# Eight expert blocks move from the one-hot steps to the routing, and VectorE makes the low parts of 39 blocks

## The reference, cut to what matters

```python
def peer_block(xb, w_q, sub_keys, expert_u, expert_v):     # xb: normed tokens x 1024
    q = (xb @ w_q).reshape(T, 8, 2, 128)
    s = jnp.einsum('thpd,hpkd->thpk', q, sub_keys)          # two lists of 128 keys for each head
    sv, si = lax.top_k(s, 16)
    cand = (sv[:, :, 0, :, None] + sv[:, :, 1, None, :]).reshape(T, 8, 256)
    cidx = (si[:, :, 0, :, None] * 128 + si[:, :, 1, None, :]).reshape(T, 8, 256)
    top_s, pos = lax.top_k(cand, 16)                        # the routing: 16 experts a head
    eidx = jnp.take_along_axis(cidx, pos, axis=-1)
    gate = jax.nn.softmax(top_s, axis=-1)
    u = jnp.take(expert_u, eidx, axis=0)
    act = jax.nn.gelu(jnp.einsum('thkd,td->thk', u, xb))
    v = jnp.take(expert_v, eidx, axis=0)
    return jnp.einsum('thk,thkd->td', gate * act, v)
```

## Time and profile before

| | us |
|---|---|
| median of 3 runs | 2854.35 (2854.25 to 2856.07) |
| the profiled execution, its own time | 2859.36 |
| its span, from the first to the last instruction | 2857.5 |
| TensorE busy | 2697.9 |
| VectorE busy | 2213.6 |
| GpSimd busy | 1298.4 |
| mean granted TensorE clock, share of full speed | 0.981 |

### The profile page before, as it was taken

One profiled execution on the slowest core, in us unless ns is written; L12 is line 12 of the kernel. 1 busy time (PEld: TensorE's weight loads), 2 busy tenths in 40 slices (PEclk: granted clock), 3 DMA queues, 4 the chain that ended last, 5 costly groups with the idle time before them and its releaser, 6 DMA issues.

```text
span 2857.5 us, 36824 instructions
## 1 busy us (share of the span) xinstructions
PE 2697.9 (94%) x14355; PEld 2240.7 (78%) x14355; DVE 2213.6 (77%) x3528; ACT 1212.2 (42%) x1802; POOL 1298.4 (45%) x827
## 2 busy tenths in 40 slices
PE   8889999999999999999999799999999999998987
PEld 4567777767767788787788799999888898777765
DVE  3688888876878977657569998883777788888975
ACT  4234444443533466733334446564333333233333
POOL 2233333332224544204444455555676766667730
PEclk9999999999999999999999899999999999999998
DMA  7321111134422221023233346677999999899961
GB/s 280 103 70 53 52 52 52 52 125 151 144 67 74 82 67 45 30 83 117 82 103 103 119 133 225 209 249 278 360 377 361 376 341 340 321 337 322 325 246 37
DMA packets 163165, 496.12 MB, mean 174 GB/s; under 512 B 15152, under 2 KB 50992, under 8 KB 162864
## 3 DMA queue, kind: packets, MB, share of 16 engines
q1 hardware_dynamic: 126128, 359.53, 37.2%
q0 software_dynamic: 36864, 134.23, 12.7%
HBM read 443.90 MB, written 49.81 MB: 173 GB/s over the span
## 4 chain that ended last, share of the span: by engine, by line
PE 50%; DVE 24%; DMA 12%; ACT 7%; issue 4%; POOL 3%; SPq 1%; DVEq 0%; ACTq 0%; POOLq 0%
PE ps L804 12%; PE ps L806 12%; PE ps L805 12%; DMA ex<-in_ev,small 4%; DMA ex<-in_urow,small 4%; DVE ex L1806 3%; PE ps L1212 2%; DVE ex L2589 2%; DVE ex L2603 2%; DVE ex L2610 2%; DVE wsp L1806 2%; PE ps L977 2%; POOL ex L2843 1%; PE ps L997 1%; DMA ring<-in_ev 1%
## 5 line engine op out<-in xcount | busy, mean ns | idle before, releaser
L2697 POOL TENSOR_TENSOR wsp<-ring,wsp 128x1024 fp32r<-128x1024 f32 x219 | 568.2, 2600 | 867.5 <-ACT wsp L1306 839.7
L804 PE MATMUL ps<-hT,wsp 128*128 128x512 f32 (+1 forms) x2040 | 780.7, 383 | 38.0 <-POOL wsp L2697 20.0
L806 PE MATMUL ps<-hT,wsp 128*128 128x512 f32 (+1 forms) x2040 | 752.4, 369 | 0.0
L805 PE MATMUL ps<-hT,wsp 128*128 128x512 f32 (+1 forms) x2040 | 752.0, 369 | 0.0
L804 PEld LDWEIGHTS ps<-hT,wsp 128*128 128x128 f32 x2040 | 388.4, 190 | 109.1 <-issue 32.1
L806 PEld LDWEIGHTS ps<-hT,wsp 128*128 128x128 f32 x2040 | 387.8, 190 | 46.7
L805 PEld LDWEIGHTS ps<-hT,wsp 128*128 128x128 f32 x2040 | 388.9, 191 | 44.0 <-issue 5.0
L1306 ACT ACTIVATE wsp<-ring 128x1024 fp32r<-128x1024 f32 x317 | 331.9, 1055 | 158.0 <-PE ps L806 80.0
L804 PE MATMUL ps<-ex 128*128 128x512 f32 x588 | 233.7, 397 | 30.4 <-DVE ex L1806 26.9
L2855 POOL DMA_INDIRECT ex<-in_ev,small x128 | 190.5, 1488 | 110.1 <-DVE ex L2610 93.1
L2855 POOL DMA_INDIRECT ex<-in_urow,small x128 | 197.1, 1540 | 88.6 <-DVE small L2603 77.3
(11 more groups left out here) (431 smaller groups left out, 4909.3 us busy)
## 6 DMA issues: line engine op xcount, KB each, us to landing
ring<-in_eu SPq DMA_DIRECT2D x128, 512.0 KB
ring<-in_ev SPq DMA_DIRECT2D x128, 512.0 KB
ring<-in_ein SPq DMA_DIRECT2D x57, 512.0 KB
gd<-oh SPq DMA_DIRECT2D x6, 4096.0 KB, 14.0
ex<-gd SPq DMA_DIRECT2D x32, 768.0 KB
ring<-in_oin SPq DMA_DIRECT2D x39, 512.0 KB
ring<-in_ada SPq DMA_DIRECT2D x30, 512.0 KB
ex<-zd SPq DMA_DIRECT2D x20, 768.0 KB, 9.9
```

The lines of the kernel that those rows point to most:

```text
L804: pe.matmul(out, W[0], R[0], start=first, stop=False)
L805: pe.matmul(out, W[0], R[1], start=False, stop=False)
L806: return pe.matmul(out, W[1], R[0], start=False, stop=last)
L2697: pool.tensor_tensor(s[:, 1, :], raw_of(i), s[:, 0, :].bitcast(F32), ALU.subtract).then_inc(pool_done, G.step("lo", i))
```

## The change

1. Eight blocks move from the one-hot steps to the routing. Before, 4 stand ahead of the first `cand` and 4 in each token block; then 4 ahead of the first step and 2 in each of the 24 steps. Now 6 stand ahead of `cand`, then 5, 5, 6 and 6 in the token blocks (28 in all instead of 20); then 5 ahead of the first step, 1 in every step, and a second in 15 of the 24.
2. The low parts of units 33 to 71 of `expert_u` (39 units, those of the blocks among the steps) go from POOL to DVE.
3. The entry for `pre` in DVE's table calls `lo_to(n)` instead of `lo_to(n + 1)` for these blocks. The call of `split_to` in `walk` is as it was.

```diff
-SOFT = 4 + 4 * 4
-HOT = 4 + 48
+SOFT = 6 + 5 + 5 + 6 + 6
+HOT = 5 + 24 + 15
...
-    for _ in range(4):
+    for _ in range(6):
         pre()
     for blk in range(4):
         order.append(("cand", blk))
         pre()
         for part in range(4):
             order.append(("best", blk, part))
-            if part in (1, 3):
+            if part:
                 pre()
         order.append(("gates", blk))
         order.append(("decode", blk))
         order.append(("look", blk))
         pre()
+        if blk > 1:
+            pre()
         order.append(("sums", blk))
         order.append(("soft", blk))
     assert z[0] == SOFT
     order.append(("oh_begin",))
-    for _ in range(4):
+    for _ in range(5):
         pre()
     for tb in range(SD // TB):
         pre()
-        pre()
+        if tb % 8 in (1, 3, 5, 6, 7):
+            pre()
         order.append(("hot", tb))
...
-                    or name == "eu" and u < NPRE * JC)
+                    or name == "eu" and u < NPRE * JC and not SOFT + 5 <= u < SOFT + HOT)
...
-"pre": lambda j, n: lo_to(n + 1)
+"pre": lambda j, n: lo_to(n if SOFT + 5 <= j < SOFT + HOT else n + 1)
```

More of the change, by code:

```diff
@@ L2678, in vector_program @@
                   "pool_in": ahead_of, "mx_begin": mx_begin, "pool_ev": pool_ev, "bc": bc, "res": res, "vc": vc,
-                  "yms": yms, "wo": wo, "wq": ahead_of, "keys": keys, "pre": lambda j, n: lo_to(n + 1), "cand": cand_,
+                  "yms": yms, "wo": wo, "wq": ahead_of, "keys": keys, "pre": lambda j, n: lo_to(n if SOFT + 5 <= j < SOFT + HOT else n + 1), "cand": cand_,
                   "best": best, "gates": gates, "decode": decode, "look": look, "soft": soft, "hot": hot, "z": z, "v": v, "gd": gd, "gact": gact, "vl": vl, "vtr": vtr,
```

## The result

The changed kernel takes 2988.68 us (median of 4 runs, 2983.84 to 2999.28); the kernel before, run with it, 2855.21 (4 runs). The ratio is 1.047, with a 95% interval of 1.044 to 1.049: slower by some 133 us. Forecast were 3006 us and a range of 2950 to 3050.

What follows compares the result with a forecast made beforehand. TensorE was taken to bound the one-hot steps, with DVE just behind, and DVE parts of the routing. The terms -13.8 + 120 + 46 gave +152 us, so 3006 us, with a range of 2950 to 3050.

Steps and rivals of the forecast that it cites:

- term 1: In the routing: the eight moved blocks fill part of TensorE's lost time there, 13.8 us gained.
- term 2: One-hot steps: rows stand behind low parts on DVE, so PE waits 4.8 or 6.0 us, 23 times; 120 us lost.
- term 3: One-hot steps: PE resumes at a slow clock after each of 23 waits, 2.0 us each; 46 us lost.
- The rival on the other side: One-hot steps: rows come early enough, PE stays full and only the routing's gain is left; 2840 us, chance 4%.
- The one where the clock stays full: One-hot steps: the waits come but the clock is not slowed; +106 us, 2960 us, chance 16%, a mixture included.
- The one where it stays at half throughout: One-hot steps: the clock stays at half, work taken as 1.85 times as long; 3070 us, chance 8%.

Runs made afterwards that it cites:

- look0: Changed kernel with VectorE's lookahead behind a block taken off for units 33 to 71: ratio 0.9955 to the kernel before, median 2848.76 us.
- pool_lo: Changed kernel with all low parts of the early blocks back on GpSimd: ratio 0.9948 to the kernel before, median 2844.89 us.
- fill2: Changed kernel with 24 idle TensorE matmuls in each of the 24 steps, before the wait for the rows: ratio 1.0368 to the kernel before, median 2964.25 us.
- dve_only: Kernel before with the low parts of its blocks 24 to 71 on VectorE, no block moved: ratio 1.0474 to the kernel before, median 2996.34 us.
- look1: Changed kernel with VectorE's lookahead of one unit instead of two, table entry lo_to(n + 1) again: ratio 1.0036 to the kernel before, median 2868.84 us.

## Why the prediction was right, point by point

| | forecast | measured |
|---|---|---|
| routing (term 1) | -13.8 | -12.3 (`look0`), -12.8 (`pool_lo`) |
| waits at the steps (term 2) | 120 | 107.6 |
| slow clock behind them (term 3) | 46 | 35 |
| sum | 152 | 130.3 inner span, 133 by the medians |

- *What bounds.* Right: TensorE full among the steps, VectorE just behind it. VectorE's sum among the steps fell (220 us in 259 to 182 in 374) and the time rose all the same, because the order on its queue is what counts.
- *Term 1.* Right in size and in its path, but for one wait that was not seen. Counted from gelu 0, the three transposes stand 70.6, 101.2 and 131.6 us behind it. The forecast had them at 1623, 1653 and 1683, which is 69.8, 99.8 and 129.8. The exponential came when it was forecast: the first `soft` starts 43.8 us behind gelu 0 (1602.04), and 1596.9 was 43.7 behind it. But VectorE waits 5.2 us there and not 10, since it arrives 38.7 us behind gelu 0 instead of 33.5. Of this delay on the way, 5.2 us, 4.05 are a second wait for ScalarE that the forecast did not have: the copy `ids` (L1683) now stands behind gelu 5 instead of gelu 3. Contention with GpSimd adds 1.1 net: the three L2510 take 6.66 us instead of 2.41, and two other instructions 3.0 less. None of this moved the sum, since the exponential comes at the same moment whenever VectorE arrives. The first two lines are the changed kernel, the third is the kernel before:

```profile
1580.66 4.57 DVE L2499 TENSOR_TENSOR pk<-pk 128x2048 bf16<-128x2048 bf16 x2 [4.05 <-ACT pk L1683]
...
1589.73 6.66 DVE L2510 TENSOR_TENSOR pk<-pk 128x2048 bf16<-128x2048 bf16 x3
...
1583.83 2.41 DVE L2507 TENSOR_TENSOR pk<-pk 128x2048 bf16<-128x2048 bf16 x3
```

- *Term 2.* The mechanism was right, link by link. A two-block step waits 4.43 us (4.8 forecast) and a one-block step 5.15 (6.0); 23 waits. The links that were too long: the gelu starts 4.20 behind the end of the matmuls instead of 4.36, and the next high-to-low link is 1.08 instead of 1.15. In the one-block step ScalarE is free 1.1 us behind the slow matmuls instead of 1.8, since its copies keep up with them.
- *Term 3.* The term that was mis-sized most. A step's own matmuls and links beside its wait and its blocks take 17.10 - 4.43 - 8.32 = 4.35 us instead of 2.83: 1.5 us for each of 23 waits, not 2.0. The mechanism was right: the matmuls start at half the clock and the block behind them does not suffer. What was off is how long the low level lasts: 2.92 us here, which costs half of that. The price had been taken from two waits in the routing, and the length of a wait does not give it: 14.2 us cost 1.6, 6.1 cost 2.7, and 4.4 and 5.2 both cost 1.5. By the figure of the Trainium skill (TensorE: Matmul & The Clock Gate, HAM oscillation) it would have been an estimated 19 us. The measured 35 lie between that and the forecast, and the measurement decides.
- *The rival on the other side* (the chain hides) did not come true in this kernel, but it is exactly what `look0` shows once the lookahead goes. The one where the clock stays full is 24 to 28 us away: `fill2` is 24 faster on the inner span and 28 by the ratios. The one where it stays at half throughout was far off, for the granted clock of the stage is 0.90. Its own sum was added up wrong as well: 2854 + 106 + 115 is 3075, not 3070.
- *Edit 3 does nothing*: no kernel was run with that edit alone undone. But the order listing shows the low parts of units n+2 in place in spite of it, `dve_only` has the same waits of 4.43 us without it, and `look0` shows what it would have given.

## What to carry to other kernels

When work moves from an idle engine to a busy one's queue, cost its place before its amount: list what stands directly ahead of the instruction that everyone waits for, and follow *that* operand's producer back. Here 49 us of low parts were affordable and cost nothing in the right place. Two units of lookahead, harmless on GpSimd, which does nothing else in this stage, cost 143 us on the engine that also makes the rows. Look for every place that issues ahead: a shared hook behind each item outvoted the table entry that was edited. And where a producer on a third engine (the exponential, and the copy `ids` that went unseen) stands behind work that is added ahead of it, it comes later too.

## What the runs showed of the hardware

- Waits of 4.4 and 5.2 us of TensorE in each step of 14 to 17 us bring the granted clock of the stretch to 0.90, and the matmuls right behind a wait (218 ns at full clock) have a median of 308. Behind all 23 waits they start at 1.2 GHz (granted 0.50 to 0.55 over the first 2.8 us) and are at or near 2.4 GHz from 3.2 us on (0.94 to 1.00). With waits of 1.4 us in 14 of the 24 steps, `look1` has its median at 218 and its longest at 237. So the cost of a wait is not in proportion: 1.4 us cost 1.4, 4.4 cost 5.9.
- Idle matmuls in the wait paid off: 576 of them, busy 103.8 us in sum, took some 28 us off. TensorE: Matmul & The Clock Gate (HAM oscillation), in the Trainium skill, describes the same pattern of a loop that starts each pass slow; the runs agree on the pattern, and lose 1.5 us in each pass where its example loses an estimated 0.83.
- With GpSimd silent, VectorE's two-input bf16 operation of 128x2048 takes 1.22 us every time, and up to 3.4 where it meets a low part on GpSimd. Even so, taking all of that contention away gained nothing in a stage that TensorE bounds (225.9 and 226.0 us).
